# The first two weight units in quarters, and an attention stage in another order

## The chip, the cores and the metric

The kernel runs on one core of a Trainium2 chip. The metric is the device time of one execution in microseconds (us). The runs shown are three timed executions of the kernel before and one profiled execution, which has a time of its own.

## The reference

Two transformer blocks in float32 on 256 tokens of width 1024. The first has two layers: a gated linear attention layer (A) and a sparse attention layer (B), each with attention over a memory of 256 rows and followed by a feed-forward layer with a short convolution (f0, f1). The second (C) has attention with a decay, a pooling branch and a gated feed-forward layer (f2). Layer B, in which the change lies, is in short:

```python
kv = (rmsnorm(x, g_kv) @ w_kv).reshape(B, T, 6, NSA_GROUPS, NSA_DH)
k_c, v_c, k_s, v_s, k_w, v_w = [kv[:, :, i] for i in range(6)]
# k_c, v_c: 15 blocks of 32 rows, each squeezed by gelu(flat @ w1) @ w2
q, gl, mq = split_cols(h @ w_in, [NSA_WIDTH, 3 * NSA_HEADS, MEM_WIDTH])
gates = jax.nn.sigmoid(gl)
# per query: softmax over the squeezed blocks, over the selected blocks and over the window, with a slope per head
out = gates0 * o_c + gates1 * o_s + gates2 * o_w
m = mem_attend(mq, mem_k, mem_v)
return jnp.concatenate([out, m], axis=-1) @ w_out
```

With 256 tokens there are four blocks to select, and the window holds every key, so both reach the same keys. A linear layer's input is the normalised x; the kernel multiplies x with the gain first and scales the result by the token's factor.

## The kernel before

**Weights in units.** All weights are a list of 1 MB units ([128, 2048] float32 each), named in the order in which they are used: Aq, Ak, Am0, Am1, ... for layer A, kvc, kvk, Bq0, kvv, ck0, ck1, Bq1, cv0, cv1, Bm0, Bm1, Bo0 to Bo3 for layer B. SP loads unit i into one of three raw buffers (`NR` = 3). ScalarE rounds it to fp32r (`cast`, L2036, the high part in `wh`), VectorE subtracts that from the raw one (`rest`, L1246, the low part in `wl`), each in two halves, counted by `w_hi` and `w_lo`. A product is three fp32r matmuls: high by high, high by low, low by high (`mm3`). Four units (ck0, ck1, cv0, cv1) are used raw in float32. SP may load unit i when unit i - 3 has its low part, or has been used, if it is a raw one. `rests(name, ahead)` and `casts(name, ahead)` do all units up to `ahead` past the named one that aren't done yet.

**Orders by hand.** Each engine has one program in a fixed order (`pe_program` for TensorE, `dve_program` for VectorE, `act_program` for ScalarE, `pool_program`, `sp_program`), and they meet by semaphores. PSUM has eight banks; a named product opens a bank, `full` marks it computed, `freed` marks it read, and the next user of the bank waits for that.

**The start.** x comes in four quarters (two chunks of 128 rows each) on SP's queue, Aq in four quarters on ScalarE's queue, Ak whole on SP's. ScalarE enters two chunks (x times gain, rounded, L2048) and casts one quarter of Aq (L2178), four times; then it casts Ak in halves. VectorE follows with the low parts (L1254, L1461). TensorE does all of Aq (`unit_f`, 8 chunks by 2 halves by 3 matmuls, 48 matmuls) and then Ak, after which come 8 narrow products (`alr`).

**Layer B, in TensorE's order.** kvc, kvk, Bq0, the gates, `nsa_scores(0)`, the values kvv in two token tiles of 24 matmuls each, `nsa_scores(1)`, the squeezing of the key blocks (`squeeze(0, ..)`, units ck0 and ck1), `nsa_turn(0)`, half of Bq1, and on. For each of four pairs of heads j there is a chain:
- `nsa_scores(j)`: TensorE multiplies queries and keys into banks 4 to 7; VectorE adds slope times distance and takes the extremes into `EB` (L1672, L1677), and frees the banks;
- `nsa_exps(j)`: ScalarE exponentiates (L2308), for two heads g;
- `nsa_probs(j)`: VectorE divides by the sums and multiplies with the gates (L1686 to L1693);
- `nsa_turn(j)`: TensorE transposes the probabilities into banks 4, 5 and 6 (12 transposes, L411), `nsa_turned(j)`: ScalarE copies them out (L2317, L2319);
- `nsa_out(j)`: TensorE multiplies them with the values `vv`, which VectorE copied out of kvv's bank (L1762).

The squeezed blocks go through `squeezed`, `gT`, `gelu` and `kvm`, and have scores and a softmax of their own (`blocks_scores`, `blocks_in` from L1706 on, `blocks_probs`). The memory's heads go through `mem_scores`, `mem_max` (L1304), `mem_exp` (L2066), `mem_probs`, `mem_turn` and `mem_out`. Bank 4 is used in turn by turn(2), `mem_scores(1, 0)` and turn(3).

Of the kernel before, what the change touches and what calls it, by code (L numbers as in the profile page):

```python
# [9 lines left out]
ALU = mybir.AluOpType  # L10
# [6 lines left out]
T = 256  # L17
# [3 lines left out]
UW = 2048  # L21
# [133 lines left out]
NR = NH = 3  # L155
# [9 lines left out]
def program(nc, ctx, w_d, x_d, mem_d, meta_d, small_d, const_d, gmask_d, nsac_d, sel_d, out_d):  # L165
# [175 lines left out]
    d_x = [count(f"d_x{i}", 16) for i in range(4)]  # L341
    d_w0 = [count(f"d_w0q{i}", 16) for i in range(3)] + d_w[:1]
    d_meta, d_gm, d_tab = count("d_meta", 16), count("d_gmask", 16), count("d_tab", 16)
# [31 lines left out]
    c_y, c_pm, c_hi = count("c_meta_turned"), count("c_meta_probs"), count("c_out_hi")  # L375
    p_sum, p_dif, p_out, p_hi, p_lo = (count("pool_" + n) for n in ("sums", "diff", "even_out", "out_hi", "even_lo"))

    used = {}
# [14 lines left out]
    def pe_program(pe, t):  # L393
# [19 lines left out]
        def unit_f(name, bank, a_h, a_l, ready, two=None):  # L413


            i = U[name]
            H, L = v3(wslot(wh, i), 256), v3(wslot(wl, i), 256)
            P = ps.open(name, bank)
            t.wait_ge(*ps.vacant(name))
            for c in range(8):  # L420
                t.wait_ge(*(w_lo0.at(c // 4) if i == 0 and c % 4 < 2 else w_lo.at(2 * S[i] + c // 4)))
# [12 lines left out]
        def part_f(name, bank, chunks, ready, a_h=XH, a_l=XL):  # L434
# [7 lines left out]
            for c in chunks:  # L442
                t.wait_ge(*w_lo.at(2 * S[i] + c // 4))
                t.wait_ge(*ready(c))
# [7 lines left out]
        def unit_wide(name, banks_, ready, blocks=(0, 1)):  # L452
# [3 lines left out]
            for j, b in zip(blocks, banks_):  # L456
# [4 lines left out]
                for c in range(8):  # L461
                    t.wait_ge(*w_lo.at(2 * S[i] + c // 4))
                    t.wait_ge(*ready(c))
                    last = mm3(P[:, 0:TM], H[:, c, o], L[:, c, o], XFH(c), XFL(c), c == 0, c == 7)
# [4 lines left out]
        def unit_t(name, bank, a_h, a_l, ready, tiles=(0, 128), turn=(0, 1)):  # L469
# [3 lines left out]
            for n, a in enumerate(tiles):  # L473
# [7 lines left out]
                for c in range(8):  # L481
                    t.wait_ge(*w_lo.at(2 * S[i] + c // 4))
                    t.wait_ge(*ready(c))
# [67 lines left out]
        def out_part(name, bank, chunks, ready, first=4, final=3):  # L551
# [6 lines left out]
            for c in chunks:  # L558
                t.wait_ge(*w_lo.at(2 * S[i] + c // 4))
                t.wait_ge(*ready(c))  # L560
# [8 lines left out]
        def down(tag, p):  # L569
# [7 lines left out]
            if p < 10:  # L577
                for j in range(2):
                    f = 2 * p + j
                    t.wait_ge(*f_l.at(22 * m + f))  # L580
                    t.wait_ge(*w_lo.at(2 * S[i] + j))
                    for o in range(8):
# [6 lines left out]
            for j in range(2):  # L589
                t.wait_ge(*f_l.at(22 * m + 20 + j))  # L590
            t.wait_ge(*w_lo.at(2 * S[i] + 1))
            for o in range(8):
# [43 lines left out]
        x_a = entered("A")  # L636
        unit_f("Aq", bank_a(), XH, XL, x_a)
        unit_f("Ak", bank_a(), XH, XL, x_a)
        P = ps.open("alr", bank_a())
# [281 lines left out]
        last.then_inc(*ps.full("gates_t"))  # L921
        unit_t("kvv", lambda: 2, CH, CL, kv_in)
        nsa_scores(1)
        squeeze(0, 0, 0)
        squeeze(0, 1)
        nsa_turn(0)
        part_f("Bq1", 1, range(0, 4), x_b)
# [16 lines left out]
        last.then_inc(*ps.full("gT"))  # L944
        nsa_turn(2)
        P = ps.open("kvm", 2)
# [9 lines left out]
        last.then_inc(*ps.full("kvm"))  # L956
        part_f("Bm0", 1, range(4, 8), x_b)
        blocks_scores(0, (7, 0))
# [275 lines left out]
    def dve_program(v, d):  # L1234
        def rest(*names, halves=(0, 1)):

            for name in names:
# [5 lines left out]
                for a in halves:  # L1243
                    s = slice(a * HW, (a + 1) * HW)
                    d.wait_ge(*w_hi.at(2 * S[i] + a))
                    v.tensor_tensor(L[:, s], src[:, s], f32(H[:, s]), ALU.subtract).then_inc(*w_lo.up(2 * S[i] + a))  # L1246

# [206 lines left out]
        QW = UW // 4  # L1454
        to[0] = 1
        for n in range(4):
            for c in (2 * n, 2 * n + 1):
                enter("A", c, xs[c], gmix0(c), XH(c), XL(c))
            q = slice(n * QW, (n + 1) * QW)
            d.wait_ge(*(w_hi.at(n // 2) if n % 2 else w_hi0.at(n // 2)))  # L1460
            last = v.tensor_tensor(wl[:, q], raw[:, q], f32(wh[:, q]), ALU.subtract)  # L1461
            last.then_inc(*(w_lo.up(n // 2) if n % 2 else w_lo0.up(n // 2)))
        rest("Ak")

# [291 lines left out]
        v.tensor_scalar(g0, g0, cn("valid", 0, 1), None, ALU.mult).then_inc(*n_gt.up(0))  # L1756
        rests("kvv", 2)
        nsa_probs(0)
        nsa_scores(1)
        d.wait_ge(*ps.ready("kvv.0"))  # L1760
# [3 lines left out]
        last.then_inc(*ps.freed("kvv.0"))  # L1764
        rests("ck0", 2)
        nsa_probs(1)
# [255 lines left out]
    def act_program(s, a):  # L2022
        def cast(*names):

            for name in names:
# [5 lines left out]
                for n in range(2):  # L2031
                    cs = slice(n * HW, (n + 1) * HW)
                    a.wait_ge(*d_w[i % NR].at(i // NR))
                    if S[i] >= NH:
                        a.wait_ge(*used[SPLIT[S[i] - NH]])
                    s.copy(H[:, cs], src[:, cs]).then_inc(*w_hi.up(2 * S[i] + n))  # L2036

# [128 lines left out]
        QW = UW // 4  # L2166
        to[0] = 1
        for n in range(4):
            s.dma_start(raw[:, n * QW:(n + 1) * QW], w_d[0][:, n * QW:(n + 1) * QW]).then_inc(*d_w0[n].up(0))
# [4 lines left out]
        for n in range(4):  # L2174
            for c in (2 * n, 2 * n + 1):
                enter("A", c, xs[c], gmix0(c), XH(c), d_x[n].at(0))
            a.wait_ge(*d_w0[n].at(0))
            last = s.copy(wh[:, n * QW:(n + 1) * QW], raw[:, n * QW:(n + 1) * QW])  # L2178
            last.then_inc(*(w_hi.up(n // 2) if n % 2 else w_hi0.up(n // 2)))
        cast("Ak")  # L2180
        for c in range(8):
# [119 lines left out]

        def nsa_exps(j):
            for g in range(2):
                n = 2 * j + g
# [227 lines left out]
    def sp_program(sp, q):  # L2532
# [9 lines left out]
        load(small[:, 0:NG], small_d[:, 0:NG], d_gain)  # L2542
        for n in range(1, 4):
            load(xt_[:, n * 512:(n + 1) * 512], x_d[:, n * 512:(n + 1) * 512], d_x[n])
        weight(1)
        load(small[:, NG:NA], small_d[:, NG:NA], d_small)
        load(cst[:, 0:NC], const_d[:, 0:NC], d_cst)
        weight(2)
        for i in range(NR, len(NAMES)):
# [22 lines left out]
            if i - NR in S:  # L2572
                q.wait_ge(*w_lo.at(2 * S[i - NR] + 1))
            if NAMES[i - NR] in WHOLE + ("Cv0", "Cv1"):
# [166 lines left out]
```

## Time and profile before

| | |
|---|---|
| runs | 903.5, 903.67, 904.66 us, median 903.67 |
| the profiled execution | 904.41 us |
| its span, first to last instruction | 902.7 us |
| TensorE (PE) busy | 893.2 us, 99% of the span |
| VectorE (DVE) busy | 647.7 us, 72% |
| ScalarE (ACT) busy | 492.0 us, 54% |
| GpSimd (POOL) busy | 44.0 us, 5% |
| DMA | 160.68 MB, mean 178 GB/s |
| TensorE's granted clock, mean | 0.998 |

All times in the rows count from the span's start. Matmuls overlap in the array, and a row's time has the way through the array in it, so what one costs among others is the distance between starts. Layer B lies between about 331 and 430 us.

### The profile page before, as it was taken

To read this page: it belongs to the slowest core of one execution; us is meant where nothing else is said; L and a number is where in the kernel's file an instruction comes from. 1 tells how busy PE (TensorE), PEld (TensorE's weight loads), DVE (VectorE), ACT (ScalarE), POOL (GpSimd) and SP (SyncE) were. 2 spreads that over 40 slices of the span, in tenths; PEclk is the share of its full clock that TensorE was granted. 3 is DMA by queue.
4 is the path that set the end of the run, shared out by engine and by line. 5 is a ranking of instruction groups with operands and counts; after the bars stand their busy time and mean duration, and the time that the engine had idled before them with its cause. 6 is when DMAs were issued, how large, how long until landed. Compare 5 with 4: busy or idle time off the path is not lost.

```text
span 902.7 us, 18665 instructions
## 1 busy us (share of the span) xinstructions
PE 893.2 (99%) x7875; PEld 866.0 (96%) x7875; DVE 647.7 (72%) x1188; ACT 492.0 (54%) x841; POOL 44.0 (5%) x50
## 2 busy tenths in 40 slices
PE   8999999999999999999999999999999999999998
PEld 7999999999999998789999999999988999999998
DVE  6887657877767689775887767677678486565664
ACT  6663555564545566674665546447437455444451
POOL 1000001000000000000100001001132000000000
PEclk9999999999999999999999999999999999999999
DMA  9643343565454543722556554654162255555541
GB/s 348 251 175 115 136 158 137 221 238 190 159 220 183 202 158 124 277 94 94 200 188 242 207 203 164 222 199 153 38 232 94 82 208 219 194 187 202 201 158 47
DMA packets 25570, 160.68 MB, mean 178 GB/s; under 512 B 2960, under 2 KB 4880, under 8 KB 6800
## 3 DMA queue, kind: packets, MB, share of 16 engines
q1 hardware_dynamic: 24912, 158.45, 47.9%
q8 instruction: 62, 1.02, 0.4%
q10 hardware_dynamic: 576, 1.05, 0.3%
q14 instruction: 20, 0.16, 0.1%
HBM read 158.18 MB, written 1.05 MB: 176 GB/s over the span
## 4 chain that ended last, share of the span: by engine, by line
PE 92%; DVE 5%; DMA 1%; ACT 1%; issue 0%; SPq 0%
PE ps L395 90%; PE ps L411 1%; DVE wl L1246 1%; DMA raw<-in_w 1%; DVE arena L1677 1%; ACT arena L2308 0%; DVE col L1254 0%; DVE arena L1693 0%; DVE arena L1976 0%; SPq L2534 0%; DVE arena L1672 0%; DVE arena L1747 0%; ACT arena L2066 0%; DVE arena L1964 0%; DVE arena L1304 0%
## 5 line engine op out<-in xcount | busy, mean ns | idle before, releaser
L1246 DVE TENSOR_TENSOR wl<-raw,wh 128x1024 fp32r<-128x1024 f32 x282 | 331.5, 1224 | 124.3 <-ACT wh L2036 124.0
L395 PE MATMUL ps<-xh,wh 128*128 128x256 f32 (+1 forms) x1264 | 352.4, 279 | 2.8 <-DVE wl L1461 1.6
L395 PE MATMUL ps<-xl,wh 128*128 128x256 f32 (+1 forms) x1264 | 350.3, 277 | 0.0
L395 PE MATMUL ps<-xh,wl 128*128 128x256 f32 (+1 forms) x1264 | 350.2, 277 | 0.0
L2036 ACT CAST wh<-raw 128x1024 fp32r<-128x1024 f32 x282 | 278.9, 1047 | 120.2 <-PE ps L395 107.9
L395 PEld LDWEIGHTS ps<-xh,wh 128*128 128x128 f32 x1264 | 237.6, 188 | 5.5 <-issue 2.3
L395 PEld LDWEIGHTS ps<-xh,wl 128*128 128x128 f32 x1264 | 237.7, 188 | 0.0
L395 PEld LDWEIGHTS ps<-xl,wh 128*128 128x128 f32 x1264 | 237.7, 188 | 0.0
L395 PE MATMUL ps<-fh,wh 128*128 128x256 f32 x528 | 145.7, 276 | 0.0
L395 PE MATMUL ps<-fl,wh 128*128 128x256 f32 x528 | 145.7, 276 | 0.0
L395 PE MATMUL ps<-fh,wl 128*128 128x256 f32 x528 | 145.7, 276 | 0.0
L395 PEld LDWEIGHTS ps<-fh,wl 128*128 128x128 f32 x528 | 99.1, 188 | 0.0
L395 PEld LDWEIGHTS ps<-fh,wh 128*128 128x128 f32 x528 | 99.1, 188 | 0.0
L395 PEld LDWEIGHTS ps<-fl,wh 128*128 128x128 f32 x528 | 99.1, 188 | 0.0
L395 PE MATMUL ps<-coh,wh 128*128 128x256 f32 x288 | 81.6, 283 | 0.0
L395 PE MATMUL ps<-col,wh 128*128 128x256 f32 x288 | 80.0, 278 | 0.0
L395 PE MATMUL ps<-coh,wl 128*128 128x256 f32 x288 | 79.9, 278 | 0.0
L2125 ACT ACTIVATE arena<-arena,small 128x256 f32<-128x256 f32 x44 | 22.4, 510 | 74.2 <-DVE arena L1376 74.0
L395 PEld LDWEIGHTS ps<-coh,wh 128*128 128x128 f32 x288 | 54.1, 188 | 0.6 <-issue 0.3
L395 PEld LDWEIGHTS ps<-coh,wl 128*128 128x128 f32 x288 | 54.2, 188 | 0.0
L395 PEld LDWEIGHTS ps<-col,wh 128*128 128x128 f32 x288 | 54.1, 188 | 0.1
L395 PE MATMUL ps<-arena 64*128 64x128 f32 (+8 forms) x382 | 39.4, 320 | 2.0 <-POOL arena L2491 2.0
(249 smaller groups left out, 1047.6 us busy)
## 6 DMA issues: line engine op xcount, KB each, us to landing
raw<-in_w SPq DMA_DIRECT2D x145, 1024.0 KB, 4.9
raw<-in_w ACTq DMA_DIRECT2D x4, 256.0 KB, 5.7
xt<-in_x SPq DMA_DIRECT2D x4, 256.0 KB, 6.7
arena<-in_mem SPq DMA_DIRECT2D x1, 1024.0 KB, 8.8
out<-xt SPq DMA_DIRECT2D x8, 128.0 KB, 1.9
arena<-in_sel SPq DMA_DIRECT2D x3, 256.0 KB, 6.1
small<-in_small SPq DMA_DIRECT2D x1, 623.0 KB, 5.8
memkv<-in_gmask SPq DMA_DIRECT2D x1, 512.0 KB, 9.4
```

Source lines behind the costliest of these rows:

```text
L395: return pe.matmul(out, lhsT, rhs, start=start, stop=stop, skip_group_check=True)
L411: return pe.transpose(out, src, cn("ident")[0:m, 0:m])
L1246: v.tensor_tensor(L[:, s], src[:, s], f32(H[:, s]), ALU.subtract).then_inc(*w_lo.up(2 * S[i] + a))
L1677: last = v.tensor_tensor_reduce(EE[:, w * 256:(w + 1) * 256], S[:, w * 256:(w + 1) * 256], dist, -slope, 3.0e38, ALU.add, ALU.min, st[:, w ...
L2036: s.copy(H[:, cs], src[:, cs]).then_inc(*w_hi.up(2 * S[i] + n))
L2125: s.activation(yb[f % 2][:, 0:T], ab[f % 2][:, 0:T], ACT.Copy, scale=sm(cw, f, f + 1)).then_inc(*f_y.up(k0 + f))
```

## The change

Two parts. At the start, Ak comes in four quarters too, loaded between the quarters of x, and the quarters of Aq and Ak are cast, split and multiplied in turn (`QUART`), with semaphores of their own. `w_low` gives the semaphore of a half of any unit. In layer B, TensorE does kvv's second token tile after the squeezing, and `nsa_turn(2)` after Bm0's second half and `kvm`; VectorE takes scores(1) before probs(0), the values' copy after Bq1's split, and Bm0's scaling before probs(3); ScalarE takes the first `squeezed` before exps(2), and turned(2) between the two heads of exps(3).

```diff
+    QUART = [(0, 0), (0, 1), (1, 0), (0, 2), (1, 1), (0, 3), (1, 2), (1, 3)]
+    def split(i, half):
+        return 2 * (S[i] - 2) + half
+    def w_low(i, half):
+        return w_lo0.at(QUART.index((i, 2 * half + 1))) if i < 2 else w_lo.at(split(i, half))
...
TensorE
-        unit_f("Aq", bank_a(), XH, XL, x_a)
-        unit_f("Ak", bank_a(), XH, XL, x_a)
+        for u, n in QUART:
+            part_f(("Aq", "Ak")[u], None if n else bank_a(), (2 * n, 2 * n + 1), x_a)
...
-        unit_t("kvv", lambda: 2, CH, CL, kv_in)
+        unit_t("kvv", lambda: 2, CH, CL, kv_in, turn=(0,))
         nsa_scores(1)
         squeeze(0, 0, 0)
         squeeze(0, 1)
+        unit_t("kvv", None, CH, CL, kv_in, turn=(1,))
         nsa_turn(0)
...
         last.then_inc(*ps.full("gT"))
-        nsa_turn(2)
+        part_f("Bm0", 1, range(4, 8), x_b)
         P = ps.open("kvm", 2)
...
-        part_f("Bm0", 1, range(4, 8), x_b)
+        nsa_turn(2)
         blocks_scores(0, (7, 0))
VectorE
-        to[0] = 1
-        for n in range(4):
-            for c in (2 * n, 2 * n + 1):
-                enter("A", c, xs[c], gmix0(c), XH(c), XL(c))
-            q = slice(n * QW, (n + 1) * QW)
-            d.wait_ge(*(w_hi.at(n // 2) if n % 2 else w_hi0.at(n // 2)))
-            last = v.tensor_tensor(wl[:, q], raw[:, q], f32(wh[:, q]), ALU.subtract)
-            last.then_inc(*(w_lo.up(n // 2) if n % 2 else w_lo0.up(n // 2)))
-        rest("Ak")
+        to[0] = 2
+        for k, (u, n) in enumerate(QUART):
+            if u == 0:
+                for c in (2 * n, 2 * n + 1):
+                    enter("A", c, xs[c], gmix0(c), XH(c), XL(c))
+            q = slice(u * UW + n * QW, u * UW + (n + 1) * QW)
+            d.wait_ge(*w_hi0.at(k))
+            v.tensor_tensor(wl[:, q], raw[:, q], f32(wh[:, q]), ALU.subtract).then_inc(*w_lo0.up(k))
...
         rests("kvv", 2)
+        nsa_scores(1)
         nsa_probs(0)
-        nsa_scores(1)
+        rests("ck0", 2)
         d.wait_ge(*ps.ready("kvv.0"))
...
         last.then_inc(*ps.freed("kvv.0"))
-        rests("ck0", 2)
         nsa_probs(1)
...
+        by_rs("Bm0", mqB_[:, 0:512], rs_[:, 0:T], 128.0 ** -0.5)
         nsa_probs(3)
-        by_rs("Bm0", mqB_[:, 0:512], rs_[:, 0:T], 128.0 ** -0.5)
ScalarE
+        for k, (u, n) in enumerate(QUART):
+            if u == 0:
+                for c in (2 * n, 2 * n + 1):
+                    enter("A", c, xs[c], gmix0(c), XH(c), d_x[n].at(0))
+            a.wait_ge(*d_wq[u][n].at(0))
+            qs = slice(u * UW + n * QW, u * UW + (n + 1) * QW)
+            s.copy(wh[:, qs], raw[:, qs]).then_inc(*w_hi0.up(k))
...
         casts("cv0", 2)
+        squeezed(0)
         nsa_exps(2)
-        squeezed(0)
         squeezed(1)
         gelu()
         casts("cv1", 2)
-        nsa_exps(3)
+        nsa_exps(3, (0,))
         nsa_turned(2)
+        nsa_exps(3, (1,))
         casts("Bm0", 2)
SP
-        for n in range(1, 4):
-            load(xt_[:, n * 512:(n + 1) * 512], x_d[:, n * 512:(n + 1) * 512], d_x[n])
-        weight(1)
+        for n in range(4):
+            if n:
+                load(xt_[:, n * 512:(n + 1) * 512], x_d[:, n * 512:(n + 1) * 512], d_x[n])
+            for k in ((), (0,), (1,), (2, 3))[n]:
+                load(raw[:, UW + k * QW:UW + (k + 1) * QW], w_d[1][:, k * QW:(k + 1) * QW], d_wq[1][k])
```

## Rows read from the trace of the kernel before

**Rows 1.** Who TensorE waited for: us in total, times, longest us

```profile
PE ps L395 <- DVE wl L1246: 1.2, 2, 1.0
```

**Rows 2.** Timeline of the start: start us, us, engine, line, what [idle before <-releaser]

```profile
7.97 0.91 ACT L2048 ACTIVATE xh<-xt,small 128x256 fp32r<-128x256 f32 x2 [1.33 <-DMA xt<-in_x]
9.31 0.91 ACT L2048 ACTIVATE xh<-xt,small 128x256 fp32r<-128x256 f32 x2
...
10.12 0.61 ACT L2178 CAST wh<-raw 128x512 fp32r<-128x512 f32 x1
10.17 0.38 PE L395 MATMUL ps<-xh,wh 128*128 128x256 f32 x1 [1.10 <-DVE wl L1461]
...
10.82 0.69 DVE L1461 TENSOR_TENSOR wl<-raw,wh 128x512 fp32r<-128x512 f32 x1
...
11.43 0.88 DVE L1254 SCALAR_TENSOR_TENSOR xl<-xt,small,xh 128x256 fp32r<-128x256 f32 x2
...
12.47 2.00 ACT L2036 CAST wh<-raw 128x1024 fp32r<-128x1024 f32 x2 [0.42 <-DMA raw<-in_w]
...
14.83 0.38 PE L395 MATMUL ps<-xh,wh 128*128 128x256 f32 x1 [0.23 <-DVE wl L1246]
...
20.49 0.64 PE L395 MATMUL ps<-xt,wn 128*32 128x256 f32 x8
```

**Rows 3.** Busy time from 7 to 12 us, with TensorE's clock, DMA share, GB/s

```profile
7.00:12.00 5.00, 3.47 (x27) 3.28 (x28) 3.83 (x9) 4.03 (x9) 1.66 (x4) 1.00 1.02 407
```

**Rows 4.** Timeline of TensorE in layer B

```profile
357.16 1.58 PE L395 MATMUL ps<-arena,memkv 64*128 64x128 f32 x16
...
360.54 1.53 PE L411 MATMUL ps<-cst,arena 128*128 128x128 f32 x12
363.05 0.35 PE L395 MATMUL ps<-xh,wh 128*128 128x256 f32 x1 [0.98 <-DVE wl L1246]
...
383.93 1.33 PE L411 MATMUL ps<-cst,arena 128*128 128x128 f32 x6 [0.23 <-DVE arena L1677]
...
391.74 0.44 PE L395 MATMUL ps<-arena 128*64 128x256 f32 x2
...
396.98 0.71 PE L411 MATMUL ps<-cst,arena 128*128 128x128 f32 x5
```

**Rows 5.** Three stretches: PE, PEld, DVE, ACT, POOL busy, granted clock, DMA share, GB/s

```profile
360.00:363.00 3.00, 2.07 (x24) 1.42 (x16) 3.00 (x12) 3.00 (x14) 0.77 (x2) 1.00 0.67 216
382.00:384.00 2.00, 1.12 (x9) 0.78 (x9) 2.00 (x15) 1.79 (x4) 0.00 (x0) 1.00 0.71 299
384.00:387.60 3.60, 3.60 (x36) 3.03 (x37) 3.13 (x8) 3.57 (x11) 0.00 (x0) 0.53 0.14 23
```

**Rows 6.** Timeline of VectorE and ScalarE in layer B

```profile
360.90 0.87 DVE L1762 TENSOR_SCALAR arena<-ps,rst 128x256 f32<-128x256 f32 x2
361.69 2.35 DVE L1246 TENSOR_TENSOR wl<-raw,wh 128x1024 fp32r<-128x1024 f32 x2
...
376.56 0.51 ACT L2308 ACTIVATE arena<-arena 128x256 f32<-128x256 f32 x1 [2.95 <-DVE arena L1677]
...
385.68 0.51 ACT L2308 ACTIVATE arena<-arena 128x256 f32<-128x256 f32 x1
...
389.21 1.04 ACT L2317 COPY arena<-ps 128x512 f32<-128x512 f32 x2
...
390.63 2.00 ACT L2036 CAST wh<-raw 128x1024 fp32r<-128x1024 f32 x2
...
390.80 0.69 DVE L1287 SCALAR_TENSOR_TENSOR memkv<-ps,rs 128x512 f32<-128x512 f32 x1
391.84 0.60 DVE L1706 TENSOR_TENSOR arena<-ps,arena 128x60 f32<-128x60 f32 x4 [0.34 <-PE ps L395]
...
394.36 0.69 DVE L1304 TENSOR_REDUCE arena<-ps 128x2 f32<-128x512 f32 x1 [0.45 <-PE ps L395]
...
395.90 0.20 ACT L2066 ACTIVATION_READ_ACCUMULATOR arena<-ps,arena 128x1 f32 x1
```

More of the change, by code:

```diff
@@ L341, in program @@
     d_x = [count(f"d_x{i}", 16) for i in range(4)]
-    d_w0 = [count(f"d_w0q{i}", 16) for i in range(3)] + d_w[:1]
+    d_wq = [[count(f"d_w{u}q{i}", 16) for i in range(3)] + [d_w[u]] for u in range(2)]
     d_meta, d_gm, d_tab = count("d_meta", 16), count("d_gmask", 16), count("d_tab", 16)
@@ L420, in unit_f @@
             for c in range(8):
-                t.wait_ge(*(w_lo0.at(c // 4) if i == 0 and c % 4 < 2 else w_lo.at(2 * S[i] + c // 4)))
+                t.wait_ge(*w_low(i, c // 4))
                 t.wait_ge(*ready(c))
@@ L442, in part_f @@
             for c in chunks:
-                t.wait_ge(*w_lo.at(2 * S[i] + c // 4))
+                t.wait_ge(*(w_lo0.at(QUART.index((i, c // 2))) if i < 2 else w_low(i, c // 4)))
                 t.wait_ge(*ready(c))
@@ L461, in unit_wide @@
                 for c in range(8):
-                    t.wait_ge(*w_lo.at(2 * S[i] + c // 4))
+                    t.wait_ge(*w_low(i, c // 4))
                     t.wait_ge(*ready(c))
@@ L481, in unit_t @@
                 for c in range(8):
-                    t.wait_ge(*w_lo.at(2 * S[i] + c // 4))
+                    t.wait_ge(*w_low(i, c // 4))
                     t.wait_ge(*ready(c))
@@ L558, in out_part @@
             for c in chunks:
-                t.wait_ge(*w_lo.at(2 * S[i] + c // 4))
+                t.wait_ge(*w_low(i, c // 4))
                 t.wait_ge(*ready(c))
@@ L580, in down @@
                     t.wait_ge(*f_l.at(22 * m + f))
-                    t.wait_ge(*w_lo.at(2 * S[i] + j))
+                    t.wait_ge(*w_low(i, j))
                     for o in range(8):
@@ L590, in down @@
                 t.wait_ge(*f_l.at(22 * m + 20 + j))
-            t.wait_ge(*w_lo.at(2 * S[i] + 1))
+            t.wait_ge(*w_low(i, 1))
             for o in range(8):
@@ L1244, in rest @@
                     s = slice(a * HW, (a + 1) * HW)
-                    d.wait_ge(*w_hi.at(2 * S[i] + a))
-                    v.tensor_tensor(L[:, s], src[:, s], f32(H[:, s]), ALU.subtract).then_inc(*w_lo.up(2 * S[i] + a))
+                    d.wait_ge(*w_hi.at(split(i, a)))
+                    v.tensor_tensor(L[:, s], src[:, s], f32(H[:, s]), ALU.subtract).then_inc(*w_lo.up(split(i, a)))
         to = [0]
@@ L2035, in cast @@
                         a.wait_ge(*used[SPLIT[S[i] - NH]])
-                    s.copy(H[:, cs], src[:, cs]).then_inc(*w_hi.up(2 * S[i] + n))
+                    s.copy(H[:, cs], src[:, cs]).then_inc(*w_hi.up(split(i, n)))
         to = [0]
@@ L2166, in act_program @@
         QW = UW // 4
-        to[0] = 1
+        to[0] = 2
         for n in range(4):
-            s.dma_start(raw[:, n * QW:(n + 1) * QW], w_d[0][:, n * QW:(n + 1) * QW]).then_inc(*d_w0[n].up(0))
+            s.dma_start(raw[:, n * QW:(n + 1) * QW], w_d[0][:, n * QW:(n + 1) * QW]).then_inc(*d_wq[0][n].up(0))
         a.wait_ge(*s_wn0.at(0))
@@ L2173, in act_program @@
         a.wait_ge(*d_gain.at(0))
[L2174 to L2180, printed above, removed]
+        for k, (u, n) in enumerate(QUART):
[5 more added lines that the diff above has]
+            s.copy(wh[:, qs], raw[:, qs]).then_inc(*w_hi0.up(k))
         for c in range(8):
@@ L2300, in gelu, with nsa_exps @@
             s.activation(gT, ps["gT"][:, 0:120], ACT.Gelu_apprx_tanh).then_inc(*ps.freed("gT"))
-        def nsa_exps(j):
-            for g in range(2):
+        def nsa_exps(j, heads=(0, 1)):
+            for g in heads:
                 n = 2 * j + g
@@ L2542, in sp_program @@
         load(small[:, 0:NG], small_d[:, 0:NG], d_gain)
-        for n in range(1, 4):
-            load(xt_[:, n * 512:(n + 1) * 512], x_d[:, n * 512:(n + 1) * 512], d_x[n])
-        weight(1)
+        QW = UW // 4
+        for n in range(4):
[3 more added lines that the diff above has]
+                load(raw[:, UW + k * QW:UW + (k + 1) * QW], w_d[1][:, k * QW:(k + 1) * QW], d_wq[1][k])
         load(small[:, NG:NA], small_d[:, NG:NA], d_small)
@@ L2572, in sp_program @@
             if i - NR in S:
-                q.wait_ge(*w_lo.at(2 * S[i - NR] + 1))
+                q.wait_ge(*w_low(i - NR, 1))
             if NAMES[i - NR] in WHOLE + ("Cv0", "Cv1"):
```

## The prediction

> **What bounds the kernel now.** I read the waits first. TensorE is the engine that the others feed: the longest wait on a weight split is 1.0 us, and two such waits make 1.2 us [rows 1]. Its loss is in a few places, and the change touches two of them, so I read those two in order of time.
>
> The start, all engines [rows 2]: the first chunk pair of Aq is multiplied, then TensorE stands for 1.10 us until 10.17, because the second quarter's low part comes late. That goes back to ScalarE, which waited 1.33 us for the second quarter of x (7.97). TensorE waits again before 14.83: Ak's weights land as a whole at 12.47, are cast and split in halves, and the 48 matmuls of Ak run from 14.83 to 20.49 (0.118 us each).
>
> The second attention stage, TensorE [rows 4]: nsa_turn(0) starts at 360.54, Bq1 only at 363.05. A turn is 12 transposes; the row has 1.53 us for them, of which the last one's way through the array overlaps what follows (an estimate of 0.25 us, as a matmul takes 0.38 there and starts every 0.12), so the transposes take about 1.3 us and TensorE stands for about 1.2 us. Later nsa_turn(2) is cut in two by VectorE, which frees its banks (second half at 383.93). The third view is the granted clock [rows 5]: 1.00 through the wait at 360 to 363 and through 382 to 384, where TensorE is busy for 1.12 of 2.00 us, then a mean of 0.53 from 384.0 to 387.6, so nearly all of it at 1.2 GHz and not 2.4. Ahead of the fall stood short matmuls (gT), a wait, six transposes and a second wait. The last view is VectorE and ScalarE in the same stage [rows 6]: from 376.56 to about 396 they form a chain that hardly rests, and TensorE is tied to it.
>
> **The start, step by step.** The change leaves x quarter 0, the gains, x quarter 1 and Aq's four quarters first in their queues, so the wait until 10.17 stays as it is: nothing of it is gained. An entry of two chunks is printed with 0.91 us, but ScalarE begins its next work 0.81 us after it (9.31 to 10.12); the same 0.1 us off the cast of a quarter (0.61) gives 0.51. VectorE takes 0.61 us for a split (10.82 to 11.43) and 0.79 us for two chunks (0.88, less the overlap) [rows 2]. In the new order ScalarE's casts end at about 9.3 (Aq 1), 9.8 (Ak 0), 11.1 (Aq 2), 11.7 (Ak 1), 13.0 (Aq 3), 13.5 and 14.0 (Ak 2, 3), and VectorE's splits follow at 10.1, 10.7, 12.2, 12.8, 14.2, 14.8 and 15.4. TensorE takes 12 matmuls, 1.42 us, for each quarter of a unit: from 10.17 it wants them at 10.2, 11.6, 13.0, 14.4, 15.8, 17.3 and 18.7. None is late, the tightest (Aq 2) has 0.8 us left. The 84 matmuls end at 10.17 + 84 x 0.118 = 20.1, against 20.49: **0.4 us gained**. Added work: four casts and four splits instead of two and two, and three DMA issues on SP; they lie under those matmuls, and VectorE ends with the splits at 15.4, 0.4 us before it ends now.
>
> Do the bytes come in time? x quarters 2 and 3 now stand behind 0.26 and 0.52 MB of Ak. At the 407 GB/s of this stretch [rows 3] that is 0.65 and 1.3 us. Now they were there by 9.31 and 10.63 at the latest, since ScalarE took them without a wait; the new order wants them at 9.8 and 11.7 and has 0.8 us to spare on TensorE. So the bounds of this part are a gain of nothing (new waits eat it up) and one of 0.4, and I take 0.4, as no quarter comes near its limit. On SP's queue Am1 and mem are issued at about 14.2 instead of 13 (the wait is now for Aq's last quarter), behind a queue that is still full; later that stage hangs on what TensorE gives out, so the gain is kept. The Trainium skill (DMA: Bandwidth & Descriptors, Rules for kernel authors) speaks against this part: for full bandwidth it wants at least 1 MiB per DMA, and Ak comes in four of 0.25 MiB. By its sum in Anatomy of one DMA (2.0 us fixed and the bytes at 436 GB/s, for DMAs that GpSimd issues) a quarter alone is an estimated 2.6 us and the four in turn 10.4. Aq's quarters in rows 2 were in flight together, and the fourth had its cast done before 12.47.
>
> **The attention stage.** Four moves.
> 1. VectorE does the copy of the values (two instructions, 360.90 to 361.69) after Bq1's split instead of before it [rows 6]. TensorE now does scores(1) between the two token tiles of kvv, so VectorE can take scores(1) ahead of probs(0) without waiting: the scores run from 357.16 to about 358.7 now [rows 4], and without the second tile (24 matmuls, 2.9 us) in front of them they are ready at 355.8. VectorE needs about 4.9 us for scores(1) and probs(0) together and ends them at 360.90, so it comes to them at 356.0, just behind. The order of its work changes, not its sum, and Bq1's split starts 0.8 us earlier. TensorE's own order has no new wait: turn(0) still starts at 360.5, and the probabilities end at 361.0. Bq1 starts at about 362.3 instead of 363.05: **0.7 us**. The values are there at 364.1; nsa_out(0) wants them at 365.2. probs(1) ends at 366.9, turn(1) wants its second half at 367.3. If that cover were gone, each would cost the difference and no more.
> 2. This 0.7 us goes down the line: Bq1 makes the queries, these scores(2), and ScalarE's exponentials begin at 376.56, after 2.95 us of waiting for VectorE's part of them [rows 6]. The weights don't hold it up: cv0 and cv1 go into the buffers that the squeezes of ck0 and ck1 free, these run 2.9 us earlier (the moved token tile), so Bm0's load behind them on SP's queue finds less ahead of it.
> 3. gT is followed by Bm0's second half (24 matmuls, 2.9 us) and kvm, then turn(2). By then VectorE has freed the banks (383.9 - 0.7 = 383.2), so both waits in turn(2) go, and **with them I expect the fall of the clock to go**. TensorE does turn(2) by 386.1 then, waits a little for VectorE's copies of kvm, which stand behind Bm1's split (2.35 us from 383.1, and 1.0 for the copies: 386.5), and with 1.9 us of blocks_scores comes to nsa_out(2) at 388.4.
> 4. Now the chain takes over. exps(3) starts at 385.68 - 0.7 = 385.0 [rows 6]. It is 3.53 us (to 389.21), in halves 1.77, with turned(2) (389.21 to 390.63, 1.42 us) between them: the second half ends at 385.0 + 1.77 + 1.42 + 1.77 = 390.0, now at 389.2. From there to blocks_in are 2.3 us now (391.84 less its 0.34 us wait, less 389.21), of which the scaling of Bm0's queries, 0.69, has moved ahead: 390.0 + 1.6 = 391.6. blocks_in ran from 391.84 to 393.91 (394.36 less 0.45), 2.07 us: 393.6. mem_max and mem_exp(1, 0) take from 394.36 to 396.10, 1.74 us: 395.3. turn(3) takes the bank that mem_exp frees: **it starts at 395.4 instead of 396.98, 1.6 us earlier**. TensorE is ready at 388.4 + 5.24 (nsa_out(2) to turn(3), 391.74 to 396.98 now [rows 4]) = 393.7, so it stands for 1.7 us here, its longest wait in the stage.
> After it TensorE leads again (the rest of Bm1 is 24 matmuls at its own pace), and 1.6 us remain to the end of the stage.
>
> The fall alone: TensorE lost about 3.6 x 0.47 = 1.7 us of work, but without it ScalarE's copies of turn(2) would still have held nsa_out(2) until 390.63, and turn(3) would have come 5.24 us later, at 395.9. **Of the 1.6 us, 1.0 is the fall that goes and 0.6 the order.**
>
> **The sum.** The profiled execution took 904.41, its span is 902.7. 904.41 - 0.4 - 1.6 = 902.4. The median of the runs is 903.67, and their values are 903.5, 903.67 and 904.66. The step of 1.0 between them is just the price of the fall, so I take it that two of the three ran without it and that the new kernel is to be set against them: the same 902.4 is 1.3 us, 0.14%, below the median. That is less than 0.2% (1.8 us), about what a measurement of this kernel can tell from no change.
>
> **The rivals.**
> - *The forecast*, 902.4, both gains and no fall of the clock. 50%.
> - *The median has the fall in it*, and the profiled run is 0.74 longer for other reasons. Then 2.0 us come off the median: 901.7, 0.22% faster. For it: the fall is in the one execution that is seen. Against: the step in the values. 20%.
> - *The clock falls at the new wait.* TensorE stands for 1.7 us before turn(3), then come 12 transposes, four matmuls, four transposes. What stood before the fall at 384 was much the same [rows 5]. Against: 1.2 us of wait behind a turn, at 361.8, left the clock at 1.00. A fall as long as that one costs dense matmuls 1.7 us: 904.1, the same as now. From 2.6 us at half clock on, the gain on the median is gone; from 6.2 us on, it is slower by 0.2% (905.5), which is the case on the other side. The Trainium skill (TensorE: Matmul & The Clock Gate, What's actually happening) has the half clock as the default and activity as what lifts it. By that rule new idleness is the danger, and the row at 361.8 alone does not exclude it. 20%, of which 5% slower.
> - *The quarters do nothing or come late.* If Ak's last quarter came 4 us later than the whole does now, TensorE would wait; up to there nothing is lost. Without the 0.4: 902.8. 10%, with 3% for a loss past 0.2% from here and from the stage's order (turned(2) ahead of the second exponentials, should it wait for turn(2)).
>
> The range: 901.3 (the median's reading, with 0.4 more of luck) to 904.2 (the fall). The likeliest case alone is 902.0 to 902.9. Faster by over 0.2%: 0.27; within: 0.65; slower: 0.08.
>
> **What the profile after would show.** Right: TensorE's first wait unchanged (about 10.2), no wait at 14.4, the alr matmuls at 20.1; Bq1 0.7 us after the turn's end and not 1.2; turn(2) in one piece; mem_exp(1, 0) as the releaser of turn(3), after some 1.7 us; granted clock 1.00 throughout. Wrong: x quarters that ScalarE waits for in the middle of the start; a wait for a bank or for probs before turn(0) or turn(1); a stretch at 0.5 of the clock behind turn(3); or the stage's end less than 1 us earlier.

## The result and the profile after

The changed kernel takes 902.37 us (median of 13 executions, 901.68 to 902.8) and the kernel before, on the same chip, 903.82 (13 executions, 903.46 to 905.39). The measured ratio is 0.9979, with a 95% interval of 0.9972 to 0.9986: 0.21% faster. (It is not the quotient of the two medians, which is 0.9984; the means, 904.11 and 902.30 us, give 0.9980.) The forecast was 902.4. The profiled execution of the changed kernel took 902.06, with a span of 900.4 and a mean granted clock of 1.000; the one before took 904.41, with 902.7 and 0.998. So 2.35 us lie between the two traces, and 1.45 between the two medians.

Lines of the changed kernel are numbered 11 higher on TensorE (395 is now 406, 411 is 422), 11 to 13 higher on the others. First the waits of TensorE after the change (us in total, times, longest).

```profile
PE ps L406 <- POOL arena L2503: 2.0, 1, 2.0
PE ps L422 <- ACT arena L2077: 1.4, 1, 1.4
PE ps L406 <- DVE wl L1474: 0.9, 2, 0.6
```

The second row is new: turn(3) waits for ScalarE's mem_exp(1, 0), once, 1.4 us. The wait for weight splits of line 1246 that was there [rows 1] has gone from the top of the list; its larger part was Bq1's. Now the start of the changed kernel, all engines (start us, us, engine, line, what, idle before and releaser).

```profile
7.06 0.91 ACT L2059 ACTIVATE xh<-xt,small 128x256 fp32r<-128x256 f32 x2 [0.52 <-DMA xt<-in_x]
...
9.54 0.39 PE L406 MATMUL ps<-xh,wh 128*128 128x256 f32 x1 [0.59 <-DVE wl L1474]
...
9.91 0.62 ACT L2191 CAST wh<-raw 128x512 fp32r<-128x512 f32 x1 [1.42 <-DMA raw<-in_w]
...
10.57 0.69 DVE L1474 TENSOR_TENSOR wl<-raw,wh 128x512 fp32r<-128x512 f32 x1 [1.09 <-ACT wh L2191]
...
20.02 1.07 PE L406 MATMUL ps<-xt,wn 128*32 128x256 f32 x16
```

The alr matmuls, which follow the last one of Ak, start at 20.02 and not at 20.49 [rows 2]: 0.47 us. The way there is another one than was forecast. x quarter 1 is taken at 7.06 instead of 7.97, TensorE's first long wait ends at 9.54 instead of 10.17, and ScalarE then stands for 1.42 us, since Ak's first quarter is there only at 9.91. Its split starts at 10.57, and TensorE waits 0.31 us for it, until 11.32.

Layer B of the changed kernel on TensorE:

```profile
360.18 1.47 PE L422 MATMUL ps<-cst,arena 128*128 128x128 f32 x12
...
361.78 0.36 PE L406 MATMUL ps<-xh,wh 128*128 128x256 f32 x1
...
384.48 1.53 PE L422 MATMUL ps<-cst,arena 128*128 128x128 f32 x12
...
387.87 1.52 PE L406 MATMUL ps<-arena 128*64 128x256 f32 x16
...
394.65 1.53 PE L422 MATMUL ps<-cst,arena 128*128 128x128 f32 x12 [1.38 <-ACT arena L2077]
```

The same stage on VectorE and ScalarE:

```profile
360.42 2.35 DVE L1258 TENSOR_TENSOR wl<-raw,wh 128x1024 fp32r<-128x1024 f32 x2
362.69 0.87 DVE L1774 TENSOR_SCALAR arena<-ps,rst 128x256 f32<-128x256 f32 x2
...
384.43 0.51 ACT L2319 ACTIVATE arena<-arena 128x256 f32<-128x256 f32 x1
...
386.20 1.05 ACT L2328 COPY arena<-ps 128x512 f32<-128x512 f32 x2
387.62 0.52 ACT L2319 ACTIVATE arena<-arena 128x256 f32<-128x256 f32 x1
...
390.88 0.59 DVE L1717 TENSOR_TENSOR arena<-ps,arena 128x60 f32<-128x60 f32 x4
...
393.58 0.47 ACT L2077 ACTIVATE arena<-ps,arena 128x256 f32<-128x256 f32 x1 [0.20 <-DVE arena L1316]
```

And its windows (PE, PEld, DVE, ACT, POOL busy, granted clock, DMA share, GB/s):

```profile
380.00:384.00 4.00, 4.00 (x40) 3.86 (x40) 4.00 (x20) 3.53 (x5) 0.00 (x0) 1.00 0.56 236
384.00:387.60 3.60, 3.60 (x65) 3.30 (x62) 3.46 (x11) 3.59 (x12) 0.00 (x0) 1.00 0.43 134
393.00:395.00 2.00, 0.62 (x6) 0.42 (x5) 1.90 (x7) 1.41 (x5) 0.00 (x0) 1.00 0.00 0
```

Bq1's split now starts ahead of the copy of the values, at 360.42 and not 361.69 [rows 6], and Bq1 follows turn(0) after 1.60 us instead of 2.51 [rows 4]. turn(2) stands in one piece at 384.48, and nsa_out(2) follows at 387.87 without a wait for its copies. TensorE is busy without a gap from 380 to 387.6 at the full clock; before, 384.0 to 387.6 had a mean of 0.53 [rows 5]. The two short rows of ScalarE at 384.43 and 387.62 open the halves of exps(3); the copies of turn(2), at 386.20, lie between them. turn(3) starts at 394.65 instead of 396.98 [rows 4]. Counted from turn(0) in each trace, the way to turn(3) is 34.47 us and was 36.44.

### The profile page after: what moved, and what is told of

It reads as the page before. It is cut to its first block, busy times and chain, and to the rows that moved or that the text cites. A ratio compares the mean times of both kernels' runs of the same rounds, so it can differ in the third digit from the quotient of the medians.

```text
span 900.4 us, 18672 instructions
## 1 busy us (share of the span) xinstructions
PE 892.1 (99%) x7875; PEld 865.3 (96%) x7875; DVE 647.9 (72%) x1190; ACT 493.5 (55%) x843; POOL 43.6 (5%) x50
## 4 chain that ended last, share of the span: by engine, by line
PE 93%; DVE 4%; ACT 2%; DMA 1%; issue 0%; SPq 0%; DVEq 0%
PE ps L406 91%; PE ps L422 2%; DVE wl L1258 1%; DMA raw<-in_w 1%; ACT arena L2319 0%; DVE col L1266 0%; ACT arena L2077 0%; DVE arena L1987 0%; DVE arena L1316 0%; ACT wh L2047 0%; DVE arena L1975 0%; DVE arena L1511 0%; DVE arena L1542 0%; ACT L2319 0%; SPq L2546 0%
```

## The experiments

Each was timed in five rounds beside the kernel before. Four shared one chip, four a second one, and three a third. A median below is compared with runs of the same chip where its ratio is given; differences between medians of two chips are good to about 0.2 us, by the scatter of the repeats. Each timed execution also has its mean granted clock. Over all three sets the kernel before was executed 100 times. In 52 the clock was 1.000 and the median 903.57 us (902.79 to 904.84); in 48 it was 0.998 or 0.999 and the median 904.77 (903.4 to 905.7). **So the clock falls in about half of the executions of the kernel before, and these take 1.2 us more.** Only the profiled executions show where in the kernel the fall stands: at 384 us in both of the kernel before [rows 5]. For all others it is the mean alone that tells of it.

### The kernel before once more

No edit: the scale for the others.

> The kernel before, unchanged, to see its clock in many executions. My theory (two of three executions ran without the fall of the clock): some executions show a mean granted clock of 1.000 and take about 903.5, others 0.998 and take 1.0 us more. The rival (the fall is in every execution, and the profiled one is longer for other reasons): 0.998 in all, and the times spread without it.

Measured: 903.81 us (11 executions), ratio 0.9995 (0.9986 to 1.0003). Four executions had the clock at 0.998 and a median of 904.37, seven had 1.000 and 903.53. Two names of one kernel differ by 0.05%, within the interval.

### The start alone

The kernel before with the start's part of the diff:

```diff
+        for u, n in QUART:
+            part_f(("Aq", "Ak")[u], None if n else bank_a(), (2 * n, 2 * n + 1), x_a)
...
+            for k in ((), (0,), (1,), (2, 3))[n]:
+                load(raw[:, UW + k * QW:UW + (k + 1) * QW], w_d[1][:, k * QW:(k + 1) * QW], d_wq[1][k])
```

> Only the start's part of the change. My theory: 0.4 to 0.5 us faster (TensorE comes to the alr matmuls at 20.0 to 20.1 instead of 20.49), 0.999 to 1.000 of before. The rival (what is gained at the start is lost before layer B, where another engine sets the end of a wait): no difference, and layer B's first turn starts at 360.5 again.

Measured: 904.65 (11), ratio 1.0001 (0.9992 to 1.0009). Eight of the 11 had the fall (0.998, median 904.75), three had not (903.01). The medians as they stand say nothing, because the mixture was another one than that of its neighbours. Among executions at 1.000 it is 0.56 us below the 903.57 of the kernel before, from three executions only. Its trace has no fall. In it the distance from turn(0) to turn(3) is 35.51 us, so the old order takes 0.93 us less than in the trace before, where the clock fell:

```profile
360.17 1.53 PE L422 MATMUL ps<-cst,arena 128*128 128x128 f32 x12
362.69 0.36 PE L406 MATMUL ps<-xh,wh 128*128 128x256 f32 x1 [0.98 <-DVE wl L1257]
...
395.68 1.47 PE L422 MATMUL ps<-cst,arena 128*128 128x128 f32 x12
```

### The attention stage alone

The kernel before with the stage's part of the diff, of which TensorE's moves and the cut of exps(3) are shown:

```diff
-        unit_t("kvv", lambda: 2, CH, CL, kv_in)
+        unit_t("kvv", lambda: 2, CH, CL, kv_in, turn=(0,))
         nsa_scores(1)
         squeeze(0, 0, 0)
         squeeze(0, 1)
+        unit_t("kvv", None, CH, CL, kv_in, turn=(1,))
...
-        nsa_turn(2)
+        part_f("Bm0", 1, range(4, 8), x_b)
...
-        part_f("Bm0", 1, range(4, 8), x_b)
+        nsa_turn(2)
...
-        nsa_exps(3)
+        nsa_exps(3, (0,))
         nsa_turned(2)
+        nsa_exps(3, (1,))
```

> Only the attention stage's part. My theory: 1.6 to 1.9 us faster than an execution before with the fall of the clock, 0.6 to 0.9 faster than one without; Bq1 0.7 us earlier, no fall, TensorE waits some 1.4 us for mem_exp(1, 0). The rival (the two parts need each other): less than half of that.

Measured: 902.78 (11), ratio 0.9985 (0.9976 to 0.9994). None of the 11 had the fall. Against the kernel before at 1.000 that is 0.8 us for the order itself; against its executions with the fall, 2.0. turn(3) waited 1.47 us for mem_exp, as in the full change.

### The waits of turn(2) filled

The kernel before, with ten useless matmuls in the places where TensorE waits before and within turn(2). They write to a bank that nobody reads at that time, and the output doesn't change.

```diff
+        filler(7)
-        nsa_turn(2)
+        nsa_turn(2, 3)
```

> The kernel before, with 7 matmuls of no use (high by high, 128x256, into a free bank) after gT and 3 more between the halves of turn(2), where TensorE waits for VectorE. Nothing else changes and no result is used. My theory: TensorE's clock stays at 1.00, turn(3) starts 1.0 us earlier than in an execution with the fall, and the time is 1.0 us below such an execution. The rival (the fall costs nothing that counts, as VectorE and ScalarE set the pace there): no fall, and the same time as before to 0.2 us, or slower by the 0.3 us that the fill may stick out.

Measured: 904.06 (11), ratio 0.9998 (0.9989 to 1.0007). Three executions had the fall (median 905.1), eight had not (903.81). That is fewer falls than 48 of 100, but three of 11 would not be rare if nothing had changed, so this is weak evidence that the waits bring the fall. I had expected none. The trace kept has no fall, so it does not show where the three stood; if they stood at 384 too, the waits are not all of it. Without a fall the filling costs 0.24 us (903.81 against 903.57).

### turn(2) back in its old place

The changed kernel, with this one exchange undone on TensorE:

```diff
-        part_f("Bm0", 1, range(4, 8), x_b)
+        nsa_turn(2)
...
-        nsa_turn(2)
+        part_f("Bm0", 1, range(4, 8), x_b)
```

> The changed kernel with turn(2) back ahead of kvm and of Bm0's second half. My theory (this move takes the waits away in which the clock falls, and little else): falls come back in a part of the executions (mean clock 0.998), such executions are 0.7 to 1.3 us longer than the changed kernel's 902.4, and the others are within 0.2 us of it, since mem_exp(1, 0) still sets turn(3). The rival (the move earns its time by the order alone): no fall in any, and all executions 0.5 us or more longer.

Measured: 902.6 (11), ratio 0.9986 (0.9977 to 0.9994), two executions at 0.998 (median 903.45) and nine at 1.000 (902.57). The waits of turn(2) are back, as TensorE's timeline of this kernel shows. Its first wait was in the kernel before:

```profile
382.82 0.88 PE L411 MATMUL ps<-cst,arena 128*128 128x128 f32 x6 [0.64 <-DVE arena L1677]
```

and both are, with turn(2) back:

```profile
382.00 0.88 PE L422 MATMUL ps<-cst,arena 128*128 128x128 f32 x6 [0.64 <-DVE arena L1688]
...
383.11 0.88 PE L422 MATMUL ps<-cst,arena 128*128 128x128 f32 x6 [0.24 <-DVE arena L1688]
```

The two waits make 0.88 us, and the kernel is still only 0.2 us above the changed one. The work behind them ended in the wait for mem_exp anyway: turn(3) starts 34.47 us after turn(0), as in the changed kernel. So the waits by themselves are nearly free. The two executions with a fall are 0.9 us dearer than the others, but two of 11 cannot be told for sure from the none of 24 of the changed kernel, and no trace shows where these falls stood.

### exps(3) in one piece

The changed kernel, with ScalarE's split undone:

```diff
-        nsa_exps(3, (0,))
+        nsa_exps(3)
         nsa_turned(2)
-        nsa_exps(3, (1,))
```

> The changed kernel with both heads of exps(3) ahead of turned(2), as before the change. My theory: nothing changes in the time (within 0.2 us). VectorE's chain to mem_exp(1, 0) could be 1.4 us earlier, but nsa_out(2) and mem_scores(1, 0) then wait 1.5 us for the copies of turn(2), so the wait only moves and turn(3) starts at 394.6 again. The rival (the split of exps(3) is a gain or a loss of its own): 0.5 us or more either way.

Measured: 903.72 (12), ratio 0.9999 (0.9991 to 1.0008). The gain is gone, and my expectation was wrong. Three executions kept the clock (median 902.73), five were at 0.998 (903.65) and four at 0.996 (905.15). TensorE's timeline and the windows (columns as above) of the profiled one, which took 904.81:

```profile
389.61 2.79 PE L406 MATMUL ps<-arena 128*64 128x256 f32 x15 [1.70 <-ACT arena L2330]
```

```profile
386.00:388.00 2.00, 1.91 (x33) 1.81 (x32) 1.80 (x5) 2.00 (x11) 0.00 (x0) 1.00 0.78 254
388.00:389.50 1.50, 0.00 (x0) 0.00 (x0) 1.36 (x5) 1.50 (x5) 0.00 (x0) 0.71 0.74 311
389.50:395.50 6.00, 5.89 (x26) 4.59 (x27) 2.81 (x11) 2.56 (x4) 0.00 (x0) 0.50 0.00 0
```

nsa_out(2) needs ScalarE's copies of turn(2). With the exponentials in one piece in front of them, TensorE is through with turn(2) and the scores of blocks and then stands for 1.70 us. In this wait the clock falls, and stays at 1.2 GHz until about 395.5. In the three executions where it does not fall the split is worth only 0.4 us (902.73 against 902.33 to 902.37). Of the nine with a fall one has a trace; the other eight show it by their mean alone.

### Only turn(2) moved

The kernel before, with the exchange on TensorE alone:

```diff
-        nsa_turn(2)
+        part_f("Bm0", 1, range(4, 8), x_b)
...
-        part_f("Bm0", 1, range(4, 8), x_b)
+        nsa_turn(2)
```

> The kernel before with one edit, on TensorE alone: turn(2) behind Bm0's second half and kvm. My theory: no fall of the clock (or in few executions), and otherwise nothing: ScalarE's chain still starts exps(3) at 385.7, so the executions take what those of the kernel before without a fall take, 903.55 to 0.2 us. The rival (the order gives 0.6 us too): 903.0. The other rival (the copies of turn(2) come late and hold up nsa_out(2), so that a new wait and a fall come there): executions of 0.998 and 904 to 905.

Measured: 904.99 (11), ratio 1.0009 (1.0 to 1.0018), and 10 of 11 executions below 1.000. By the first theory, that the waits of turn(2) bring the fall and their removal removes it, hardly any should have been. Timeline of TensorE and windows of this kernel:

```profile
387.07 1.96 PE L395 MATMUL ps<-arena,memkv 64*128 64x15 f32 x32
...
390.74 1.12 PE L395 MATMUL ps<-arena 128*64 128x256 f32 x4 [1.71 <-ACT arena L2319]
```

```profile
385.60:389.00 3.40, 3.40 (x49) 3.17 (x44) 2.65 (x10) 3.40 (x16) 0.00 (x0) 1.00 0.50 159
389.00:390.70 1.70, 0.03 (x2) 0.00 (x0) 1.40 (x5) 1.70 (x6) 0.00 (x0) 0.86 0.71 284
390.70:393.50 2.80, 2.76 (x17) 1.81 (x17) 2.45 (x9) 1.92 (x3) 0.00 (x0) 0.50 0.03 15
```

The waits of turn(2) are gone, and a longer one stands 7 us further on. In the profiled execution the clock falls within it; of the other falls only the mean is known. In front of the wait are transposes, the 24 narrow matmuls of kvm and the 32 of blocks_scores with 15 columns each.

### All of x ahead of Ak

The changed kernel, with the quarters of Ak issued behind the whole of x:

```diff
-            for k in ((), (0,), (1,), (2, 3))[n]:
+            for k in ((), (), (), (0, 1, 2, 3))[n]:
```

> The changed kernel with Ak's four quarters loaded behind all of x instead of between its quarters. My theory (the transfers of one queue land in the order of their issue, at about 400 GB/s): Ak's first quarter lands 1.2 us later than the 9.9 of the changed kernel, TensorE waits 1.2 to 1.5 us instead of 0.3 for it, and the start's gain is lost (+0.8 to 1.2 us, about 903.4). The rival (the order of issue matters little, as the transfers share the engines): within 0.2 us of the changed kernel.

Measured: 902.94 (11), ratio 0.9986 (0.9978 to 0.9995), all at 1.000: 0.6 us above the changed kernel. I had expected 0.8 to 1.2. The start of this kernel:

```profile
11.10 0.62 ACT L2191 CAST wh<-raw 128x512 fp32r<-128x512 f32 x1 [2.28 <-DMA raw<-in_w]
...
12.49 0.38 PE L406 MATMUL ps<-xh,wh 128*128 128x256 f32 x1 [1.22 <-DVE wl L1474]
```

Ak's first quarter is cast at 11.10 and not at 9.91; TensorE waits 1.22 us for it, and the alr matmuls start at 21.17. This order of multiplying needs the interleaved order of loading; without it the start is slower than that of the kernel before.

### The wait for mem_exp taken away

The changed kernel with turn(3) ahead of the scores whose exponentials it waited for, and these in the bank that is free by then. VectorE and ScalarE follow in the same order.

```diff
-        mem_scores(1, 0, 4, mqB, qB)
         part_f("Bm1", 1, range(0, 4), x_b)
         nsa_turn(3)
-        mem_scores(1, 1, 0, mqB, qB)
+        mem_scores(1, 0, 0, mqB, qB)
         blocks_turn(7)
         part_f("Bm1", 1, range(4, 8), x_b)
+        mem_scores(1, 1, 0, mqB, qB)
...
-        mem_exp(1, 0, scB)
         nsa_turned(3)
+        mem_exp(1, 0, scB)
```

> The changed kernel with Bm1's first half and turn(3) ahead of mem_scores(1, 0), which goes to bank 0, so that turn(3) no longer waits for mem_exp(1, 0); mem_scores(1, 1) follows Bm1's second half, and mem_max(1, 0) and mem_exp(1, 0) go behind blocks_probs and turned(3). My theory: the wait of 1.4 us goes, turn(3) starts 2.4 us earlier, but the memory's first head is later by 0.5 to 1 us and takes a part back at mem_out(1, 0): 0.5 to 1.0 us faster than the changed kernel. The rival (the chain through the memory's heads sets the stage's end, so the wait only moves): the same time to 0.2 us.

Measured: 901.98 (11), ratio 0.9976 (0.9967 to 0.9985), all at 1.000. turn(3) starts without a wait at 392.62, 2.0 us earlier (2.5 counted from turn(0)), but only 0.4 us reach the end, less than the 0.5 to 1.0 expected:

```profile
400.43 0.47 ACT L2077 ACTIVATE arena<-ps,arena 128x256 f32<-128x256 f32 x1 [3.00 <-DVE arena L1316]
...
402.42 2.36 DVE L1258 TENSOR_TENSOR wl<-raw,wh 128x1024 fp32r<-128x1024 f32 x2
...
403.87 1.13 PE L406 MATMUL ps<-arena,memkv 128*128 128x256 f32 x4 [0.39 <-ACT arena L2086]
```

mem_out(1, 0) now waits at 403.87 for ScalarE, and the next memory head's maximum stands on VectorE behind the 2.36 us split of the weights at 402.42. The wait was moved, not removed.

### The changed kernel once more

No edit, on the third chip, beside the two kernels of that set.

> The changed kernel, unchanged, beside the next two on one chip, and for its clock in many executions. My theory: no fall in any execution, 902.3 to 902.5. The rival (the 1.4 us wait before turn(3) makes the clock fall now and then): a few executions with 0.998 and some 904.

Measured: 902.33 (11), ratio 0.9978 (0.997 to 0.9987), all at 1.000. With the 13 of the first timing that makes 24 executions of the changed kernel, and the clock fell in none.

### That version with the weight split cut in two

The kernel with mem_exp's wait taken away, with Bo1's cast (the one that `casts("Bm1", 2)` does) earlier on ScalarE and VectorE's split of Bo1 in two halves around the maximum:

```diff
-            mem_probs(1, 1, scB)
-            rests("Bm1", 2)
+            rest("Bo1", halves=(0,))
...
         mem_max(1, 2, scB)
+        rest("Bo1", halves=(1,))
...
-        mem_exp(1, 1, scB)
         casts("Bm1", 2)
+        mem_exp(1, 1, scB)
```

> The kernel with Bm1 and turn(3) ahead of mem_scores(1, 0), and Bo1's preparation out of the way of the memory's first head: ScalarE casts it before mem_exp(1, 1), where it waited 3.0 us, and VectorE splits the first half before the copies of the heads and the second half behind mem_max(1, 2). My theory (the chain through VectorE and ScalarE to mem_max(1, 2) is what took the gain back): mem_max(1, 2) 0.6 us earlier, 0.5 us off the 902.0 of the kernel without this. The rival (the waits between the heads of the memory go on and eat it): 0 to 0.2 us.

Measured: 901.21 (5, four at 1.000 and one at 0.999), ratio 0.9968 (0.9956 to 0.9981), the best of all: 0.32% below the kernel before. That is 0.8 us below the 901.98 of the kernel without this, though from five executions and on another chip. VectorE's timeline:

```profile
401.67 1.22 DVE L1258 TENSOR_TENSOR wl<-raw,wh 128x1024 fp32r<-128x1024 f32 x1
...
404.62 0.69 DVE L1316 TENSOR_REDUCE arena<-ps 128x2 f32<-128x512 f32 x1 [0.42 <-PE ps L406]
```

One half, 1.22 us, stands ahead of the maximum, which comes at 404.62 and waits for TensorE instead of holding it up; in the kernel without the cut it came at 405.90. Of these 1.28 us, 0.57 stood already at turn(0) (360.04 against 360.61), so the stage itself gives 0.7, where 0.6 was expected.

## Why the prediction came out right, step by step

**The base.** The prediction took the step of 1.0 us between the values of the three runs for the price of the fall, and that two of three ran without it. The hundred executions say 1.2 us and about one in two. The reading was right, and so was to set the new kernel against a median without the fall: 903.57 in those executions, where 903.67 was taken. The figure of 902.4 is partly luck, though. It was the profiled execution's 904.41 less 2.0; by the prediction's own parts, a median without the fall should lose only 0.4 and 0.6, which gives 902.7. The measured 902.37 is lower because the order gave more than 0.6, as told below. The rival that the median has the fall in it is out. Still, on the third chip the median of the kernel before was 904.56: with a mixture near half and half the median of one set falls on either side, and the ratio of one set (1.0001 for the start alone, with the fall in eight of 11) can hide half a microsecond.

**The start, 0.4 us.** The total was right. The timed executions give 0.56 (start alone, three executions at 1.000) and 0.41 (902.78 for the stage alone less 902.37, over two chips). By the traces it is less: the alr matmuls start at a mean of 20.42 in five kernels with the old start (20.11 to 20.79) and of 20.19 in seven with the new one (19.87 to 20.51), so a single pair, 0.47, says little about it. But that total is luck, as the working was wrong in two terms that cancel. "The wait until 10.17 stays as it is": it ended at 9.54, and in all six other traces with the new start between 9.30 and 9.93, because x's second quarter is taken at 6.88 to 7.40 and no longer at 7.64 to 8.02 wherever ScalarE waits for it. Why it lands earlier no run settled. The kernel with all of x ahead of Ak has it at 7.39, but its first entry is early too: from the first entry to the second it takes 2.31 us, against 1.64 to 1.94 in the five kernels with quarters of x and Ak in turn where ScalarE waits there, and 2.32 to 2.74 with the old start. So the place in the queue is not excluded. And "none is late": the cast of Ak's first quarter was forecast to begin at 9.3, began at 9.91, and cost TensorE 0.31 us. From the end of the first long wait to the alr matmuls it is 10.48 us now and was 10.32, against 9.9 forecast. So behind that wait nothing was gained in this pair of traces, and the whole 0.47 is its earlier end. The step that failed is the one on the bytes, which asked only whether x could wait for Ak, and never when Ak's own first quarter lands. The kernel with x first shows what that omission is worth in full, 0.6 us. The estimate that the prediction worked out by the Trainium skill (DMA: Bandwidth & Descriptors, Anatomy of one DMA), 2.6 us for a quarter alone and 10.4 for four in turn, is for DMAs that GpSimd issues, and this trace is no test of it. SP issued Ak's quarters between 2.11 and 6.06, among other loads, and each took 8.1 us (median) from issue to landing, so they were in flight together.

**Bq1, 0.7 us.** It was 0.9: 1.60 us from turn(0) to Bq1 instead of 2.51. The split started right behind the probabilities, and the values, now copied at 362.69, were there in time. That this goes down the line was right: exps(3) began at 384.43, forecast 385.0 and 385.68 before; 0.36 of these 1.25 us are the start's.

**turn(2) and the clock.** "Both waits in turn(2) go, and with them I expect the fall of the clock to go." The waits went and so did the fall, in all 24 executions, but **the "with them" is the step that is not borne out.** Moved alone, turn(2) loses its waits and a fall comes in 10 of 11 executions, in the trace kept at the next wait. Left in its old place with the rest of the change, it keeps both waits, and a fall comes in only 2 of 11. What is shown is the part of the cut of exps(3): it brings the copies of turn(2) ahead of the second half of the exponentials, so that nsa_out(2) finds them done, and without it there are falls in 9 of 12 executions instead of none of 24. That the exchange is needed beside it is not shown, as two falls in 11 may be chance, and the other moves of the stage (VectorE's order, `squeezed` ahead of exps(2)) were never tried alone. The prediction had the numbers for it (TensorE at nsa_out(2) at 388.4, the copies done at 388.2 with the cut) but put the cut on the cost side of the chain alone.

**The chain and turn(3), 1.6 us.** It was 2.33 in absolute time, of which 0.36 came with turn(0), so 1.97 in the stage. At its end the last four transposes start at 412.66 where they started at 414.83: 2.17, and 1.7 to 1.8 without the part of the start (0.36 by turn(0), 0.47 by the alr matmuls). The forecast's parts were 1.0 for the fall and 0.6 for the order. Measured were 1.2 for the fall, and for the order 0.8 in the timed executions (903.57 less 902.78) and 1.04 in the traces (35.51 less 34.47). By the timed executions the terms were undersized by 0.2 each. In the traces the fall is 0.93 (36.44 less 35.51), so the sum, 2.0 by both ways against the forecast's 1.6, is surer than its parts. mem_exp(1, 0) released turn(3), as forecast, after 1.38 us instead of 1.7. The chain ran 0.7 us ahead of the forecast from blocks_in on (390.88 against 391.6). So the profiled execution, 902.06, came out 0.3 below the sum of 902.4.

**The rival of the clock falling at the new wait** did not happen: the window at 393 to 395, which holds this wait of 1.4 us, has TensorE busy for 0.62 us of 2 and the clock at 1.00, and the mean clock was 1.000 in all 24 executions. It was a fair rival, though, as such a fall at a wait of 1.7 us, some 6 us earlier, was one edit away (exps(3) in one piece). That the quarters do nothing is out as well (0.4 to 0.6).

**What is left open.** The waits filled with useless matmuls had three falls in 11 executions against 48 in 100, and turn(2) put back had two: these numbers are too small to say how much of the old fall is due to its two waits, how much to the short matmuls ahead of them, and whether moving turn(2) was needed at all. Which executions get the fall, with the same program and the same times up to it, is not told by any trace.

## What to carry to other kernels

Before a wait on TensorE is moved, write down what stands in front of it and which engine's result comes next: a move that ends one wait is finished only when the copies behind it are scheduled too, or the wait comes back one group later and may bring the half clock with it. Where the times of one kernel fall into two groups, sort the executions by their granted clock before comparing, and price a change once within each group and once for the share of executions that leave the slower one. When a load is cut in pieces so that work can begin on the first, ask first when that first piece lands, and put it ahead of what is wanted later.

## What the runs showed that was not expected

- A wait of 1.70 or 1.71 us was enough for the clock to fall: behind turn(2), kvm and blocks_scores (transposes and matmuls with 15 to 64 columns) it fell there in the one trace of each of two kernels, of which 9 of 12 and 10 of 11 executions have a fall somewhere. With the wait of 1.38 to 1.47 us behind the 24 matmuls of Bm1 with 256 columns each, no execution has one: none of the 24 of the changed kernel, of the 11 of the stage alone and of the 11 with x first. No run has the two waits at the same length, so whether the 0.2 to 0.3 us or the work in front makes the difference stays open. The Trainium skill (TensorE: Matmul & The Clock Gate, What's actually happening) has activity as what releases the full clock. The direction agrees, as both falls come in a wait of TensorE.
- TensorE was busy for 3.40 of 3.40 us (385.6 to 389.0) just ahead of such a fall, by the records. A busy share near 1 in front of a wait is no sign that the clock is safe.
- Once down, it stayed down for about 3.4 us in the trace before (a mean of 0.53 over the 3.6 us of [rows 5]), and for almost 7 us (388.6 to 395.5) in the one with exps(3) in one piece, with TensorE busy for 5.89 of the last 6.00 us. The longer fall costs more: 905.15 at a mean clock of 0.996 against 902.73 at 1.000, 2.4 us.
